# A two-layer hybrid decoder step: six of the eight down-projection tiles paired, 8 of 22 row blocks as seven products for eight, with token sums kept where the residual lies

## The reference

```python
h = x + RMSNorm_post(Mixer(RMSNorm_pre(x)))
gate, up = split(RMSNorm_pre2(h) @ w_gate_up)      # 1024 x 5632
f = (silu(gate) * up) @ w_down                     # 2816 x 1024
y = h + RMSNorm_post2(f)
```

## Time and profile before

| | us |
|---|---|
| median of 3 runs (lowest, highest) | 1375.78 (1375.32, 1376.69) |
| the profiled execution | 1374.25 |
| its span, first to last instruction | 1372.5 |
| PE busy in the span | 1354.4 |
| DVE, ACT, POOL busy | 1017.3, 674.9, 117.8 |

### The profile page before, as it was taken

One profiled execution on the slowest core, in us unless ns is written; L12 is line 12 of the kernel. 1 busy time (PEld: TensorE's weight loads), 2 busy tenths in 40 slices (PEclk: granted clock), 3 DMA queues, 4 the chain that ended last, 5 costly groups with the idle time before them and its releaser, 6 DMA issues.

```text
span 1372.5 us, 29091 instructions
## 1 busy us (share of the span) xinstructions
PE 1354.4 (99%) x12134; PEld 1333.1 (97%) x12134; DVE 1017.3 (74%) x1615; ACT 674.9 (49%) x1360; POOL 117.8 (9%) x175
## 2 busy tenths in 40 slices
PE   9999999999999999999999999999999999999997
PEld 8999999999999999999989999999999999999996
DVE  7746796768999888644586468958689988886545
ACT  5235554547545445544542364635575445455542
POOL 0001221000000000022100002110000000000220
PEclk9999999999999999999999999999999999999998
...
GB/s 211 109 107 78 68 111 110 47 70 78 101 116 101 116 93 108 136 220 237 147 62 108 109 62 101 109 94 32 82 95 94 111 106 101 114 95 156 218 233 102
DMA packets 70116, 155.91 MB, mean 114 GB/s; under 512 B 20672, under 2 KB 24128, under 8 KB 69984
## 3 DMA queue, kind: packets, MB, share of 16 engines
...
...
## 4 chain that ended last, share of the span: by engine, by line
PE 89%; DVE 7%; issue 1%; ACT 1%; DMA 0%; DVEq 0%; ACTq 0%; SPq 0%
PE PS L677 50%; PE PS L1231 8%; PE PS L1232 8%; PE PS L1233 8%; PE PS L683 5%; DVE Wl L1884 1%; DVE hT L1922 1%; DVE Xl L1901 1%; DVE mT L1921 1%; PE PS L873 1%; DVE actL L2463 1%; PE PS L845 1%; PE PS L857 1%; PE PS L1019 1%; PE PS L855 1%
## 5 line engine op out<-in xcount | busy, mean ns | idle before, releaser
L1299 ACT ACTIVATE Wh<-stage 128x1024 fp32r<-128x1024 f32 x143 | 151.1, 1058 | 288.7 <-PE PS L677 265.1
L677 PE MATMUL PS<-Xh,Wh 128*128 128x260 f32 x1376 | 285.5, 289 | 1.7 <-DVE Wl L1946 1.0
L677 PE MATMUL PS<-Xh,Wl 128*128 128x260 f32 x1376 | 276.8, 283 | 0.0
L677 PE MATMUL PS<-Xl,Wh 128*128 128x260 f32 x1376 | 276.4, 282 | 0.0
L1884 DVE TENSOR_TENSOR Wl<-stage,Wh 128x1024 fp32r<-128x1024 f32 x143 | 174.7, 1223 | 100.3 <-ACT Wh L1299 99.6
L677 PEld LDWEIGHTS PS<-Xh,Wh 128*128 128x128 f32 x1376 | 211.4, 189 | 5.3 <-DVE Wl L1946 1.8
L677 PEld LDWEIGHTS PS<-Xl,Wh 128*128 128x128 f32 x1376 | 211.9, 188 | 0.0
L677 PEld LDWEIGHTS PS<-Xh,Wl 128*128 128x128 f32 x1376 | 211.8, 188 | 0.0
L1231 PE MATMUL PS<-XU,hiB 128*128 128x260 f32 x448 | 126.8, 283 | 0.0
L1231 PE MATMUL PS<-XU,hiA 128*128 128x260 f32 x448 | 126.8, 283 | 0.0
L1232 PE MATMUL PS<-XU,hiB 128*128 128x260 f32 x448 | 126.6, 283 | 0.0
...
## 6 DMA issues: line engine op xcount, KB each, us to landing
stage<-w_slabs SPq DMA_DIRECT2D x143, 512.0 KB, 3.3
raw<-w_slabs SPq DMA_DIRECT2D x136, 256.0 KB, 2.9
dst<-state_ret POOLq DMA_DIRECT2D x32, 256.0 KB, 3.6
dst<-state_gdn POOLq DMA_DIRECT2D x32, 256.0 KB, 4.2
vb<-v_tmp POOLq DMA_DIRECT2D x32, 256.0 KB, 4.9
out_gdn_sample<-dst POOLq DMA_DIRECT2D x16, 256.0 KB, 3.5
out_ret_sample<-dst POOLq DMA_DIRECT2D x16, 256.0 KB, 3.5
hT<-x_t SPq DMA_DIRECT2D x3, 520.0 KB, 6.4
```

The costliest lines, as they stand in the source:

```text
L677: ins = mm(pj(slot)[:, a], w[:, ws, pos, :], x[:, a, :], start=first and w is Wh and x is xh, stop=last and w is Wl)
L1299: A(Wh[:, G % NW], stage[:, G % NS], ACT.Copy).then_inc(s["hi_split"], 1)
```

## The change

The down tiles 1 to 6 form three pairs. Of the 22 row blocks, 8 to 11 (`LEFT`) and 12 to 15 (`RIGHT`) are taken with both tiles of a pair and both token halves as a 2 x 2 product of 2 x 2, in Winograd's form: seven products of four blocks (`down_products`), 84 matmuls for 96. The other 14 blocks of both tiles are added on the same PSUM banks (`down_rests`). Tiles 0 and 7 stay as they were, but tile 0 takes the blocks in the order 0-7, 16-19, 8-15, 20, 21.

The products need sums of weight blocks and of activations. DVE makes four weight sums a pair from two loaded slabs (`down_sums`, 512 wide each); they go through `hi` and `lo` as slabs of their own, `sums`, `stash` and, of half width, `last`, so a pair has eight slab steps, of which six are loaded and four hold seven blocks. A layer has 30 steps where it had 22.

The token sums (`token_sum`, `token_high`, `token_low`, 1040 wide each) are made once a layer and serve all three pairs. Two operands, T1 and T2, are made in the Strassen rounds 12 to 15 and lie where the residual `hT` lies (`T12`). For that POOL stores `hT` to DRAM (`h_tmp`) once the mixer's part is added, and ACT issues the load back when the products of the third pair are done. Two more, T3 and T4, lie in the space of `Xh` (`T34`), which is in use until the Strassen rounds end, and are made in the first down tile. All sums read `actF`, blocks 8 to 15.

DVE's posts of a pair (`down_post`: U2, U3 and the sum on `m5`) and ACT's copies of products 1 and 3 (`copy_p1`, `copy_m5`) link the products: PE's product 5 (t3) waits for U2, product 4 (b22) for the copy of product 2. `down_tile` adds these to the PSUM banks in place of a plain copy. The state groups stand five to a pair and one behind.

```diff
...
+    SIDE = 3
+    PER_PAIR = 8
+    ND = 2 * SIDE + PAIRS * PER_PAIR
+    SLABS = S_DN + ND
...
+                pool.dma_start(h_tmp[l], hT[:]).then_inc(s["tmp_stored"], 16)
...
+                for i, j in enumerate(DOWN_ORDER):
+                    if i % 8 == 0:
+                        wait_slab(l, S_DN + i // 8)
+                    pe.wait_ge(s["act_ready"], l * FT + i + 1)
+                    ins = mm6(0, ring(i // 8), i % 8, actH[:, j], act_low(j), i == 0, i == FT - 1)
...
+                    for i, (x, bank, fresh) in enumerate(((b11, 2, True), (b21, 0, True), (t1, 1, True), (t2, 3, True), (b22, 1, False), (t3, 3, False), (t4, 2, True))):
+                        if i % 2 == 0:
+                            wait_slab(l, S_DN + d0 + i // 2)
+                        if p == 0 and x >= t1:
+                            pe.wait_ge(s["xu_rest"], l * X_STEPS + X_SUMS + (T_LO1, T_LO2, T_LO3, T_LO4)[x - t1])
+                        if x == b22:
+                            pe.wait_ge(s["gate_half"], l * GATED + Q * HALVES + p * D_COPIES + D_M5)
+                        elif x == t3:
+                            pe.wait_ge(s["post_done"], l * POSTED + Q * POSTS + p * D_POSTS + D_U2)
+                        elif x == t4:
+                            pe.wait_ge(s["gate_half"], l * GATED + Q * HALVES + p * D_COPIES + D_P1)
...
+                def token_high(i):
+
+                    act.wait_ge(s["xu_rest"], l * X_STEPS + X_SUMS + (T_1, T_2, T_3AGAIN, T_4)[i])
+                    if i == 3:
+                        act.wait_ge(s["act_ready"], l * FT + DOWN_ORDER.index(FT - 2) + 1)
+                    to, src = (T12[:, i, 0], F12[:, i, 1]) if i < 2 else (T34[:, i - 2, i - 2], F34[:, i - 2, 3 - i])
+                    A(to, src, ACT.Copy).then_inc(s["t_high"], 1)
...
+                        if q in (Q - 4, Q - 2):
+                            token_high((q - Q + 4) // 2)
...
-                        act_high(8, 2)
+                        act_high(16, 2)
                         gate_second(q)
-                        act_high(10, 2)
-                        act_high(12, 2)
+                        act_high(18, 2)
                         hi(G0 + S_DN + 2)
-                        for j in range(14, FT - 2, 2):
+                        for j in range(8, 16, 2):
                             act_high(j, 2)
                         act_high(FT - 2, 1)
                         act_high(FT - 1, 1)
+                        token_high(2)
+                        token_high(3)
...
+                for i in range(ND - NW):
                     hi(G0 + S_DN + i + NW)
...
+                    p, j = divmod(i - SIDE, PER_PAIR)
+                    if j == PER_PAIR - 1:
+                        if p + 1 < PAIRS:
+                            copy_p1(p + 1)
+                        keyed(5 * p + 5)
+                    elif i < SIDE:
+                        continue
+                    elif j == 0:
+                        copy_m5(p)
+                        square_down(2 * p)
...
+                    elif j == 3:
+                        if p + 1 == PAIRS:
+                            act.wait_ge(s["p_done"], (l + 1) * MADE)
+                            act.dma_start(hT[:], h_tmp[l]).then_inc(s["x0_loaded"], 16)
+                    elif j != 2:
+                        keyed(5 * p + (1 if j == 1 else j - 2))
...
+            def down_sums(l, p):
+
...
+                for g in (G, G + 1):
+                    dve.wait_ge(s[f"slab{g % NS}_loaded"], loads(g) * 16)
+                wait_free(dve, G + 1 - NW)
+                V.tensor_tensor(s1, a21, a22, ALU.add).then_inc(s["w_rest"], 1)
+                dve.wait_ge(s["w_rest"], done + D_S1)
+                V.tensor_tensor(s2, s1, a11, ALU.subtract).then_inc(s["w_rest"], 1)
+                V.tensor_tensor(s3, a11, a21, ALU.subtract).then_inc(s["w_rest"], 1)
+                dve.wait_ge(s["w_rest"], done + D_S2)
+                V.tensor_tensor(s4, a12, s2, ALU.subtract).then_inc(s["w_rest"], 1)
 
             for l in range(DEPTH):
...
                     if k0 == 0:
+                        if n == 3 and a == 0:
...
+                def token_sum(i):
+
+                    left, right = LEFT[0], RIGHT[0]
+                    b11, b12, b21, b22 = (actF[:, j:j + 4, a] for j in (left, right) for a in range(2))
...
+                        dve.wait_ge(s["act_new"], l * FT + right + 4)
+                        dve.wait_ge(s["tmp_stored"], (l + 1) * 32)
+                        dve.wait_ge(s["ffn_round"], l * ROUND + KT)
+                    elif i in (T_2, T_4):
+                        dve.wait_ge(s["xu_rest"], l * X_STEPS + X_SUMS + i - 1)
+                    elif i == T_3AGAIN:
+                        dve.wait_ge(s["p_done"], l * MADE + Q * UN)
+                    to, x, y, op = {T_1: (F12[:, 0, 1], b12, b11, ALU.subtract), T_3: (F12[:, 1, 1], b22, b12, ALU.subtract),
+                                    T_2: (F12[:, 1, 1], F12[:, 1, 1], b11, ALU.add), T_3AGAIN: (F34[:, 0, 1], b22, b12, ALU.subtract),
+                                    T_21: (F34[:, 1, 0], b21, b11, ALU.subtract), T_4: (F34[:, 1, 0], F34[:, 1, 0], F34[:, 0, 1], ALU.subtract)}[i]
+                    V.tensor_tensor(to, x, y, op).then_inc(s["xu_rest"], 1)
+
+                def token_low(i):
+                    dve.wait_ge(s["t_high"], l * 4 + i + 1)
+                    T_, F_, lo_ = (T12, F12, 1) if i < 2 else (T34, F34, 3 - i)
+                    u = i % 2
+                    V.tensor_tensor(T_[:, u, lo_], F_[:, u, lo_], plain(T_[:, u, 1 - lo_]), ALU.subtract).then_inc(s["xu_rest"], 1)
 
...
+                        if Q - 5 <= q < Q - 2:
+                            token_sum((T_1, T_3, T_2)[q - Q + 5])
+                        elif q == Q - 2:
+                            token_low(0)
...
                 lo(G0 + S_DN + 1)
-                rest_act(8, 2)
+                token_low(1)
+                rest_act(16, 2)
                 post(Q - 1, C21)
-                rest_act(10, 2)
+                rest_act(18, 2)
                 gated(Q - 1)
-                rest_act(12, 2)
                 lo(G0 + S_DN + 2)
-                for j in range(14, FT - 2, 2):
+                for i in (T_3AGAIN, T_21, T_4):
+                    token_sum(i)
+                for j in range(8, 16, 2):
                     rest_act(j, 2)
                 rest_act(FT - 2, 1)
                 rest_act(FT - 1, 1)
...
+                for i in range(ND - NW):
+                    p, j = divmod(i - SIDE, PER_PAIR)
+                    if j == 1 and i > SIDE:
+                        down_post(p, D_U2)
+                    elif j == 2 and i > SIDE:
+                        down_post(p, D_U3)
+                    if (i + 2 - SIDE) % PER_PAIR == 0 and i + 2 < ND - SIDE:
+                        down_sums(l, (i + 2 - SIDE) // PER_PAIR)
                     lo(G0 + S_DN + i + NW)
...
+                    if i == SIDE - 2:
+                        token_low(2)
+                        token_low(3)
+                    if i == SIDE - 1:
+                        down_tile(0)
+                    if i < SIDE:
+                        continue
+                    if j == 0:
+                        new_state(5 * p)
+                    elif j == 1:
+                        down_post(p, D_E)
+                        add_squares(3, 2 * p)
+                        new_state(5 * p + 1)
+                    elif j in (4, 5, 6):
+                        if j == 5:
+                            down_tile(2 * p + 1)
+                        new_state(5 * p + j - 2)
+                        if j == 5:
+                            add_squares(3, 2 * p + 1)
+                    elif j == PER_PAIR - 1:
+                        down_tile(2 * p + 2)
+                        if p + 1 == PAIRS:
+                            new_state(5 * p + 5)
+                add_squares(3, KT - 2)
...
```

338 lines of the change are left out of this document (240 added, 98 removed).

## The result

| | median us | range | runs | profiled run | its span |
|---|---|---|---|---|---|
| before | 1376.07 | 1375.32 to 1376.69 | 4 | 1374.25 | 1372.5 |
| after | 1401.01 | 1395.73 to 1404.22 | 4 | 1395.73 | 1393.9 |

The ratio is 1.0182 (95% interval 1.0166 to 1.0197): the change makes the kernel 25 us slower. The forecast was 9.5 us slower, 1385.3, with a range to 1395. The direction was right, the size missed by 15.7 us, and the time is outside the range. The profiled run of after is the fastest of its four, so the traces show 21.4 of the 25 us.

A forecast was written before the change was run, and what follows sets the result against it. TensorE, busy 99%, was taken to bound the kernel. From 1375.8 us, 72 removed matmuls save 8.6 and waits in the first tile and pair add 18.1, giving 1385.3; range 1379 to 1395.

The forecast's parts named there:

- (b): First down tile, layer 0: with the added DVE work, PE waits 0.4 us, then 4.8 us at place 12.
- (c): First pair's operands: PE waits 1.6, 0.9, 0.5 and 1.25 us, the last for U2 before product 5.
- place 12: Twelfth place in PE's block order, first down tile: due 561.8, starts 566.6 after DVE's sums and rest_act(8), 4.8 us wait.
- rival C: First down tile: the long wait may halve PE's clock, up to 4.2 us a layer, 1393.7 us; chance 0.13.
- the wait for slab 3: PE's 1.6 us wait before product 0; would hide a half clock lasting fewer than some 16 matmuls.
- term (d): Second and third pairs: sums made during the pair ahead, cost taken as 0; if missed, up to 2.3 us a layer.
- rival D: Second and third pairs: ACT held at a state's load, next slab late; 2 to 4 us a layer, about 1391; chance 0.10.
- the sum of DVE's work "in 30.2 us": Second and third pairs: DVE's work, some 20 us a pair, fits in 252 matmuls, 30.2 us.
- term (e): Residual's store and reload, 2080 KB and 13 to 26 us each: hidden, reload needed 31 us after issue.
- "slabs have over 5 us to spare there": Last third of the down stage, beside the reload: slab loads have over 5 us to spare, the states less.
- term (a): Strassen rounds 12 to 15: three token sums and a low part added, PE cost taken as 0, else 1 us a layer.

The follow-up runs named there:

- z1: Changed kernel with other orders in the first down tile: DVE's token sums, PE's blocks (20, 21 before 8 to 15), ACT's slab 3 high part earlier; 1393.10 us.
- y1: Changed kernel with the sixteen state groups behind the copy of the middle block and the tiles' squares and high parts, whole reload kept; 1394.46 us.
- v1: w2 with the sixteenth state group behind the square of tile 6 on ACT and behind its sum on DVE; 1381.75 us.
- w2: y2 with z1's order in the first tile and the residual's store in four parts; 1383.59 us.
- z4: Changed kernel with state groups from step 3 on, six to a pair, DVE each one step later than ACT, whole reload; 1447.32 us.
- x1: Changed kernel without the residual's reload; VectorE sets hT to zero instead, so the residual is missing from the output; 1392.51 us.
- y2: y1 with the residual's reload in four transfers of 520 KB in four neighbouring ACT steps; 1392.63 us.
- w3: w1 without the residual's reload, VectorE setting the residual's tile to zero; 1390.03 us.
- w1: w2 with the state groups of each buffer three ACT steps apart, never in the step ahead of a copy; 1389.81 us.
- x4: Changed kernel with the residual's reload in four parts of 520 KB, one a slab step, state groups unmoved; 1400.49 us.

## Why the prediction was right and wrong

**Right: the first tile and pair, terms (b) and (c).** The wait at place 12 is 4.51 us at 566.60 (forecast 4.8 at 566.6), product 5 starts at 585.45 (585.3), the second pair at 608.53, within 0.3 us of what the terms give. z1 shows that the cause named, the fixed order, is the cause: with the orders of DVE, ACT and PE's blocks changed product 5 comes 4 us sooner. Which of the three orders counts for how much it does not tell.

**Right for another reason: the clock, rival C.** It did fall, and for 25 matmuls, more than the 16 that the wait for slab 3 was to hide: product 0 came at 576.50, 1.1 us late. By product 5 nothing of it was left, since DVE's row did not wait for PE. The rule of the Trainium skill ("TensorE: Matmul & The Clock Gate", "HAM oscillation — how this bites in real kernels"), that an array left waiting starts the next burst slow, agrees with this trace: 0.50 from 566.6 to 572.0, then 0.96. The way back, which no row had shown, took some 5 us. What the forecast lacked is that a shorter wait elsewhere can have a like price: 1.82 us of waiting at 680.83 and 18 matmuls in the 4.2 us behind it, which at full rate need 2.2 us. Not every wait had it: z1's 1.54 and 1.22 us left the clock at 1.00.

**Wrong: term (d), "I take 0", with rival D at 2 to 4 us and 0.10.** D named the mechanism: ACT held at a state's load, the next thing behind it late. In the tiles it was small (0.45 and 0.56 us on m in the profiled run, both in the third pair; the second has no wait), but it moved the last group from 1.2 to 7.8 us into the last tile, and y1 and v1 show the price: y1 alone takes 6.5 us off, and the last group's move in v1 another 1.8 (which the intervals of w2 and v1 don't quite tell apart). The step that failed is the sum of DVE's work "in 30.2 us": it counted busy time of DVE and left out ACT's waiting, which is on no busy list. An estimate from z4's round: five groups in two buffers are 2.5 rounds of 9.7 us for each buffer, 24 of a pair's 30 us, which leaves ACT hardly a place where a group doesn't wait.

**Wrong: term (e), "hidden at both bounds".** The transfer was even shorter than the lower bound (12.2 us, forecast 13 to 26) and the first residual addition doesn't wait for it. But "slabs have over 5 us to spare there" failed: the 448 KB slab beside it held ACT for 8.44 us, 5.21 without the reload, and though PE did not wait for that slab, the groups behind it came late. x1 prices the reload at 8.5 us in after's order. This and the 6.5 us of the groups overlap, as y2, which treats both, gains 8.4: the loss is where the two meet. In four parts with the groups at w1's steps it costs nothing that shows (w3 against w1); in parts alone (x4) it costs as before.

**Wrong: term (a), in part.** The Strassen rounds of layer 0 show no new wait, so the added sums cost nothing there. Layer 1's first rounds do wait, and 1.5 us are lost, by the ring as it seems, a side of the change that wasn't costed.

**The sum.** Forecast 9.5 us; in the profiled run 21.4, of it tiles 0 to 6 12.4 (forecast 9.5), last tiles 7.8, layer 1's start 1.5. The rest to 25 lies in the other three runs, 3.5 to 8.5 us above the profiled one at clocks of 0.989 and 0.990. Where it lies in them no trace shows; that it is the groups' timing fits y1 (spread 0.2 us) and z1, which left the groups alone (9.5 us), less well w1 (5.7 us). Of the 15.7 us that the forecast missed, y2 takes off 8.4 and v1's last step some 1.8; 1.5 are layer 1's start, and about 4 stay without a run that removes them, most of them in the last tile of layer 0. The range was too short for the same reason as the sum: C and D were priced each alone, though in the last tile it is D's wait that brings the half clock.
